# One indirect DMA for u and v of a retrieval slot, and v summed by token through 64x64 blocks of TensorE

## The reference, cut to what matters

```python
e_flat = experts.reshape(PEER_BLOCK, -1)          # 128 expert numbers a token (8 heads x 16)
u = jnp.take(expert_u, e_flat, axis=0)            # rows of 1024 floats
vv = jnp.take(expert_v, e_flat, axis=0)
act = jax.nn.gelu(jnp.einsum('td,tkd->tk', xb, u), approximate=False)
coef = (gate * act).astype(vv.dtype)
return jnp.einsum('tk,tkd->td', coef, vv)         # sum over the 128 experts of a token
# y = LayerNorm(ALPHA * x1 + PEER(x1))
```

## Time and profile before

| | us |
|---|---|
| median of 3 executions | 3767.22 |
| span of the profiled execution | 3749.1 |
| outside its span, against the median | 18.1 |

### The profile page before, as it was taken

The page is one execution under the profiler, slowest core; times in us unless marked ns, Lnnn a source line. Parts: engine busy times, 40 slices in busy tenths (PEclk is TensorE's granted clock), DMA queues, the critical chain, the costliest instruction groups (busy, mean ns, idle before and its releaser), DMA issues.

```text
span 3749.1 us, 32963 instructions
## 1 busy us (share of the span) xinstructions
PE 2448.0 (65%) x10668; PEld 1113.4 (30%) x10668; DVE 2504.2 (67%) x6614; ACT 412.7 (11%) x824; POOL 2132.7 (57%) x2180
## 2 busy tenths in 40 slices
PE   7893894656566656665566676667665555765558
PEld 5462472233123312331233232323222222431112
DVE  5188689679856886688658865887587434683331
ACT  1211211100110011001100121002100111000000
POOL 0043225666666666666566656666666556747665
PEclk8896896778668777886777778777777777768889
DMA  9998999999999999999899989999999999989998
GB/s 337 347 340 301 365 397 331 379 368 400 372 369 391 405 361 344 391 410 358 314 389 402 371 335 368 408 370 361 367 410 395 413 414 403 364 294 377 368 370 324
DMA packets 374156, 1385.50 MB, mean 370 GB/s; under 512 B 44697, under 2 KB 55577, under 8 KB 362585
## 3 DMA queue, kind: packets, MB, share of 16 engines
q0 software_dynamic: 313344, 1140.99, 79.2%
q1 hardware_dynamic: 40384, 143.04, 10.3%
q10 hardware_dynamic: 20256, 99.35, 6.9%
HBM read 1369.97 MB, written 80.18 MB: 387 GB/s over the span
## 4 chain that ended last, share of the span: by engine, by line
DVE 26%; issue 14%; PE 12%; another core or an unknown queue 11%; POOL 11%; DMA 10%; ACT 2%; ACTq 0%; POOLq 0%; DVEq 0%
DVE t L1057 11%; PE psum L1409 6%; POOL t L597 6%; DMA t<-in_expert_v,t 6%; POOL t L582 5%; DMA t<-in_expert_u,t 4%; DVE t L1003 2%; DVE t L1001 2%; DVE t L1004 2%; DVE t L1002 1%; PE psum L1271 1%; PE psum L1295 1%; DVE t L1000 1%; DVE t L1030 1%
## 5 line engine op out<-in xcount | busy, mean ns | idle before, releaser
L1409 PE MATMUL psum<-t,t 128*32 128x512 f32 x4352 | 1238.8, 786 | 729.1 <-DMA t<-in_expert_v,t 526.5
L582 POOL DMA_INDIRECT t<-in_expert_u,t x1088 | 1060.5, 975 | 923.2 <-DVE t L1057 456.8
L597 POOL DMA_INDIRECT t<-in_expert_v,t x1088 | 1072.0, 985 | 675.2 <-issue 296.7
L1057 DVE CUSTOM_DVE_ANT_0 t<-psum,t 128x1024 f32<-128x1024 f32 x928 | 1116.4, 1220 | 338.6 <-DMA t<-in_expert_u,t 260.8
L1409 PEld LDWEIGHTS psum<-t,t 128*32 128x32 f32 x4352 | 257.0, 130 | 1522.2 <-issue 1472.2
L1363 PE MATMUL psum<-t,t 128*128 128x128 f32 (+1 forms) x2304 | 314.8, 302 | 31.1 <-ACT t L736 23.6
L1363 PEld LDWEIGHTS psum<-t,t 128*128 128x128 f32 x2304 | 306.5, 217 | 80.0 <-issue 52.0
L1057 DVE CUSTOM_DVE_ANT_0 t<-t,t 128x1024 f32<-128x1024 f32 x160 | 194.5, 1222 | 168.4 <-DMA t<-in_expert_u,t 151.4
L1251 PE MATMUL psum<-t,t 128*128 128x128 f32 (+2 forms) x768 | 262.1, 501 | 7.5 <-DMA t<-in_xT 6.5
L921 DVE SCALAR_TENSOR_TENSOR t<-t,t,t 128x128 f32<-128x128 f32 x840 | 237.9, 345 | 0.2
L1271 PE MATMUL psum<-t,t 64*128 64x512 f32 (+3 forms) x192 | 118.9, 744 | 110.7 <-issue 60.6
(11 more groups left out here) (141 smaller groups left out, 1865.7 us busy)
## 6 DMA issues: line engine op xcount, KB each, us to landing
t<-in_wq_t ACTq DMA_DIRECT2D x63, 1024.0 KB
out<-in_cache_k_win SPq DMA_DIRECT2D x8, 4080.0 KB
out<-in_cache_v_win SPq DMA_DIRECT2D x8, 4080.0 KB
t<-in_w_in_t ACTq DMA_DIRECT2D x44, 512.0 KB, 7.9
t<-in_kc_t SPq DMA_DIRECT2D x8, 2560.0 KB
t<-in_vc_t SPq DMA_DIRECT2D x8, 2560.0 KB
t<-in_expert_u,t POOLq DMA_INDIRECT x1088
t<-in_expert_v,t POOLq DMA_INDIRECT x1088
```

The costliest lines, as they stand in the source:

```text
L582: pool.indirect_dma_start(u_buf[:, k % U_RING, :], None, I["expert_u"][0], bass.IndirectOffsetOnAxis(ap=idn[t % 2][:, s:s + 1], axis=0)).t ...
L597: pool.indirect_dma_start(v_buf[:, k % V_RING, :], None, I["expert_v"][0], bass.IndirectOffsetOnAxis(ap=idT[t % 3][:, tau:tau + 1], axis=0 ...
L1057: dve.tensor_tensor_reduce(out=u_buf[:, k % U_RING, :], in0=x1P if banked else x1[t % 3][:, :], in1=u_buf[:, k % U_RING, :], scale=1.0, sc ...
L1409: last = pe.matmul(bank[half][32 * j:32 * j + 32, :], zt[:, (GROUPS * t + g) % Z_RING, j, :], v_buf[:, k % V_RING, half * 512:(half + 1) * ...
```

## The change

`arrays["expert_uv"]` holds u and v of an expert side by side in HBM, rows of 8 KB. One indirect DMA a slot brings both for 128 tokens (1 MB), one token a partition. There is one ring for both, of 9 buffers of 8 KB a partition; during tile 0 only 4 of them, since the space of the others still holds the operands of the projection. A buffer comes free when TensorE has summed v of its pair of slots.

As token t's v row now lies on partition t, the sum over slots needs no reduction over partitions: the weights are diagonal. `weigh` (VectorE) writes for each slot of a pair a 128x64 tile, two stacked 64x64 identities scaled per partition by the gelu of the dot and by the gate. `values_pair` (TensorE) adds v times these weights: the blocks are 64x64, rows 0 to 63 to output partitions 0 to 63 and rows 64 to 127 to 64 to 127. In tiles 1 to 6, pairs 8 to 59, the odd slot's two blocks are crossed (rows 0 to 63 to outputs 64 to 127 and the reverse), into the two banks that are free there, and one matmul with a swap matrix puts them back at the tile's end. Gelu is taken pair by pair on ScalarE, two steps before `weigh` at the latest; `weigh` stands 2 steps, `values_pair` 3 steps behind the pair's odd slot. v of a tile is finished at the start of the next stage, the residual follows at step 6, and the stages end with a short one, n = 9. x1 has two buffers instead of three and no copy in PSUM; all dots read it from SBUF. Tile 0 has 49 dots in stage -1. The v coefficients of the first gates are taken head by head. `idT`, `coef`, the transposes for them and a round trip of the sample convolution through HBM go away. The space set aside for descriptors shrinks to 4096 bytes a partition.

```diff
+RING, FIRST_RING = 9, 4
+Z_RING = 3
...
+def slots_at(n, q):
+    early = EARLY * (PH - 1)
+    if n < 0:
+        lo, hi = (min(max(q + j - ROUTE_AT - ROUTE_STEP, 0), early) for j in range(2))
+    elif n == 0:
         lo, hi = (early + (q + j) * (SLOTS - early) // SLOTS for j in range(2))
     elif n < PT:
         lo, hi = q, q + 1
...
+        def spot(t, s):
+            if t == 0:
+                return s % FIRST_RING, s // FIRST_RING
+            k = (t - 1) * SLOTS + s
+            before = SLOTS // FIRST_RING if k % RING < FIRST_RING else 0
+            return k % RING, before + k // RING
...
+            def gather(t, s):
                 if s % TOP == 0 and t < PT:
                     pool.wait_ge(a_route, PH * t + s // TOP + 1)
                 elif s == 0:
                     pool.wait_ge(id_up, 16)
...
+                r, use = spot(t, s)
+                if t == 0:
+                    if s >= FIRST_RING:
+                        pool.wait_ge(pv, pair(0, s - FIRST_RING) + 1)
+                else:
+                    k = (t - 1) * SLOTS + s
+                    if k >= RING:
+                        pool.wait_ge(pv, pair(1, k - RING) + 1)
...
+                pool.indirect_dma_start(ring[:, r, :], None, I["expert_uv"],
+                                        bass.IndirectOffsetOnAxis(ap=idn[t % 2][:, s:s + 1], axis=0)).then_inc(landed[r], 16)
...
+            def gelu(t, p):
+                act.wait_ge(a_dot, SLOTS * t + 2 * p + 2)
+                d_ = dots[t % 2][:, 2 * p:2 * p + 2]
                 act.activation(d_, d_, ACT.Gelu).then_inc(a_gelu, 1)
...
             def dot(t, s):
-                k = ku(t, s)
-                dve.wait_ge(gu[k % U_RING], 16 * (k // U_RING + 1))
-                banked = t in P_TILES and s >= P_FROM
+                r, use = spot(t, s)
+                dve.wait_ge(landed[r], 16 * (use + 1))
                 if s == 0:
                     dve.wait_ge(x1_done, 2 * (t + 1))
...
+                dve.tensor_tensor_reduce(out=ring[:, r, 0:D], in0=x1[t % 2][:, :], in1=ring[:, r, 0:D], scale=1.0,
                                          scalar=0.0, op0=ALU.mult, op1=ALU.add, accum_out=dots[t % 2][:, s:s + 1]).then_inc(a_dot, 1)
...
+            def weigh(t, p):
+                k = PAIRS * t + p
+                dve.wait_ge(a_gelu, k + 1)
                 if k >= Z_RING:
                     dve.wait_ge(pv, k - Z_RING + 1)
+                for j in range(2):
+                    s = 2 * p + j
+                    dve.tensor_scalar(zt[:, k % Z_RING, j, :], ident2[:, :], dots[t % 2][:, s:s + 1], gtn[t % 2][:, s:s + 1],
+                                      ALU.mult, ALU.mult).then_inc(zt_ready, 1)
...
+                        q = 4 * g + i
+                        for t, p in pairs_at(n, q, 2):
+                            weigh(t, p)
+                        for s in slots_at(n, q):
+                            dot(max(n, 0), s)
+                        if n >= 1 and q == RESIDUAL_AT:
+                            residual(n - 1)
...
+                pe.wait_ge(zt_ready, 2 * (k + 1))
+                for half in range(2):
+                    for j in range(2):
+                        r, _ = spot(t, 2 * p + j)
+                        vv = ring[:, r, D + half * 512:D + (half + 1) * 512]
+                        if t == PT:
+                            last = pe.matmul(MAIN[t][half][0:NS, :], zt[:, k % Z_RING, j, :], vv, start=(p == 0 and j == 0), stop=(p == w - 1 and j == 1))
+                        elif aux and j:
+                            for a in range(2):
+                                last = pe.matmul(AUX[t][half][NS - NS * a:P - NS * a, :], zt[NS * a:NS * a + NS, k % Z_RING, j, :], vv[NS * a:NS * a + NS, :],
+                                                 start=(p == AUX_PAIRS.start), stop=(p == AUX_PAIRS.stop - 1))
+                        else:
+                            for a in range(2):
+                                last = pe.matmul(MAIN[t][half][NS * a:NS * a + NS, :], zt[NS * a:NS * a + NS, k % Z_RING, j, :], vv[NS * a:NS * a + NS, :],
+                                                 start=(p == 0 and j == 0), stop=(p == w - 1 and j == 1 and t not in AUX_TILES))
+                last.then_inc(pv, 1)
```

More of the change, by code:

```diff
@@ L140, in u_slots_at, with place, pairs_at @@
         lo, hi = q, q + 1
+    elif n == PT:
+        lo, hi = (max(0, q + j - SAMPLE_LAG) * (SLOTS // 2) // (SLOTS - SAMPLE_LAG) for j in range(2))
     else:
-        lo, hi = (max(0, q + j - 4 * LAG) * (SLOTS // 2) // (SLOTS - 4 * LAG) for j in range(2))
+        lo, hi = 0, 0
     return range(lo, hi)
+def place(n, q):
+    return SLOTS * (n + 1) + q
+PAIR_PLACE = {}
+for _n in range(-1, TILES):
+    for _q in range(SLOTS):
+        for _s in slots_at(_n, _q):
+            if _s % 2:
+                PAIR_PLACE.setdefault(place(_n, _q), []).append((max(_n, 0), _s // 2))
+def pairs_at(n, q, lag):
+    return PAIR_PLACE.get(place(n, q) - lag, [])
 def rows(n):
@@ L533, in store_y @@
                 sp.wait_ge(y_done, t + 1)
[L534 removed]
+                sp.dma_start(y_o[t * P:t * P + rows(t), :], x1[t % 2][0:rows(t), :]).then_inc(y_out, 16)
             projected_loads()
[L537 removed]
+            for n in range(TILES + 1):
                 m = n + 1
@@ new lines, in gather @@
+                if t == 0:
[5 more added lines that the diff above has]
+                        pool.wait_ge(pv, pair(1, k - RING) + 1)
+                    elif k < FIRST_RING:
+                        pool.wait_ge(pv, pair(0, SLOTS - FIRST_RING + k) + 1)
+                    elif k == FIRST_RING:
+                        pool.wait_ge(proj_done, len(UNITS))
+                        pool.wait_ge(glu_done, 3 * CT)
+                        for i in range(2):
+                            pool.wait_ge(q_out[i], 64)
@@ L612, in _ @@
+                pool.indirect_dma_start(ring[:, r, :], None, I["expert_uv"],
+                                        bass.IndirectOffsetOnAxis(ap=idn[t % 2][:, s:s + 1], axis=0)).then_inc(landed[r], 16)
+            for t in range(TILES):
+                for s in range(slots(t)):
+                    gather(t, s)
         @block.scalar
```

471 lines of the change are left out of this document (179 added, 292 removed).

## The result

The changed kernel takes 4054.57 us (median of 4 executions, 4042.86 to 4059.81) where the kernel before took 3772.76 beside it (3766.46 to 3785.14): ratio 1.0745, 95% interval 1.0717 to 1.0773. It is slower, as forecast, but by 282 us where 123 were predicted, and it lies above the range of 3790 to 3990 and above 4030 too. The profiled execution has a span of 4052.3 us, 303.2 over the earlier trace rows.

What follows compares the result with a forecast made beforehand. Steady tiles were taken as bound by transfers, VectorE close behind. 329 + 8 - 36 - 5 - 169 = +127 gave a span of 3876 us, median 3894, said as 3890; likeliest case 3790 to 3990, 8 in 10 3705 to 4030.

Steps and rivals of the forecast that it cites:

- Direction and place: Whole kernel: slower, chance 0.72, because tile 0's loop through four buffers loses 329 us.
- The sum: Tile 0's chain: a pair's v sum on TensorE takes 2.2 us at the granted clock.
- the landing: Tile 0's chain, gather to landed data: 7.0 us in stage -1, 8.5 us in stage 0.
- Clock: TensorE in tile 0: the granted 0.87 of the kernel before was used to price the v sum.
- Stage 0: Tile 0's second stretch: one-pair chain 13.2 us, two-pair 15.2; 415 us in place of 274, +141.
- Tiles 1 to 6: Steady tiles: 8 KB rows save 7.7 us a tile, 1.7 us is lost, together -36 us.
- The ring is no loss: Tiles 1 to 6: nine buffers suffice, as the loop takes about 14 us where four pairs last 21.
- Tile 7: Tile 7: -7.7 us for 8 KB rows, about +3 where routing fills VectorE, together -5 of 495.
- The end: From tile 8's first dot to the end of the span: 204 us in place of 373, -169.
- Rival 1: Whole kernel not slower: tile 0 loses under 200 us and the DMA gains more; 3635 or 3700 us, chance 0.20.
- Rival 3: v sums: straight blocks do not run side by side, +1.9 us in tile 0's chain; 4010 us, chance 0.12.
- the tenth of a microsecond: Tile 0's chain: dots reading x1 from SBUF slow a GpSimd gather by 0.1 us.

Runs made afterwards that it cites:

- experiment 2: Changed kernel, but in tile 0 the v sum leaves out the odd slot of each pair, 8 records instead of 16: 3964.53 us.
- experiment 6: Changed kernel plus six zero-weight TensorE matmuls ahead of each wait for the weights of pairs 1 to 24 of tile 0, in stage -1: 4040.71 us.
- experiment 12: Changed kernel with the last pass of the projection summing only one of eight k steps: 4046.06 us.
- experiment 5: Changed kernel with tile 0 slot by slot: each slot weighed, summed and its buffer freed by itself; 3774.60 us, ratio 1.0557 to the kernel before.

## Why the prediction was wrong, step by step

- **Direction and place: right.** Tile 0's loop through four buffers is the loss, with the predicted order and releasers. The DMA share is 0.49 in stage -1 where I had said about 0.6. Tile 0 took 909.7 us, over even the 906 that all the upper bounds together gave.
- **The sum, the step that failed.** "The v sum: eight matmuls of 512 columns ... four sets of two: 1.9 us, or 3.6 at half clock." I read the x16 of the earlier trace rows as sixteen matmuls, and they are the records of eight. So each of the four sets of two takes two records one after the other, 0.86 us instead of 0.43: 3.65 us a pair at the full clock, 6.55 nearly all at half, 5.59 on the mean of stage -1. The earlier trace rows was misread too: its four records start at 1210.08, 1210.10, 1210.51 and 1210.53, two by two 0.43 us apart, which is the full clock. Against 2.2 the sum is 3.4 us longer in 24.5 pairs, +83 us; the landing, 5.85 instead of 7.0, takes 28 back. The net +55 is the stage's miss (368 against 314). In experiment 2 the sum with 8 records takes tile 0 to 817 us and the time to 3964.53, inside the range.
- **Clock.** I carried the granted 0.87 of before over to a TensorE that now idles 144 of the stage's 368 us. It was 0.78, and experiment 6 shows the idling to be the cause. Taken at 0.87 in the way of the prediction, 3.65 us would be 4.2; so of the 3.4 us about 2.0 are the records and 1.4 the clock (an estimate), 49 and 34 us of the stage.
- **Stage 0, +119** (541.7 for 415 + 8, the restart being 9.8 for 8). "Three pairs take both once: 28.4 / 3 = 9.5 us." The share was near (15 of 35 pairs behind the even dot), both chains were too short: 17.9 and 11.1 us a pair for 13.2 and 7.6. In the 15 pairs the sum takes 4.27 us for 2.2 and the landing 7.43 for 8.5, and the weights wait 3.21 us for TensorE, which works on the projection and the front, where the prediction had 0.3 for a hand-over and gave no reason to leave the queue out. Half the sum is worth 43 us in this stage (experiment 2). How the other 76 divide was not shown: experiment 12 takes 1.5 us a pair off that wait, and the stage gains only 9 us, because sum and landing become longer.
- **Tiles 1 to 6, -17 instead of -36.** "The ring is no loss" was wrong: one buffer less costs 29 us a tile, a sum one step earlier gives 8.3. What works against it is the rate where buffers are free, 412 GB/s in tile 8 and not 382. That the two errors have opposite signs and so bring the total near the forecast is luck; what each is worth in these tiles was not taken apart. The crossed sums are mostly hidden as said, though a pair takes 1.95 us at the full clock and 2.45 on the mean, not 1.0 to 1.9.
- **Tile 7, +10 instead of -5.** TensorE has 382 us of 505 instead of 294 of 495, since 64 straight pairs have 8 records more than priced. That this is what made the tile longer is argued, not shown: experiment 5 has 494.8 us with the same code for it. Sums and weights a step earlier bring it to 487 to 491.
- **The end, -201 instead of -169:** 155.8 us to the last dot instead of 188 (176 and 12 of idle DMA). The rate was higher and the DMA did not idle (share 1.00); 9 of the 64 gathers were issued before tile 8's first dot. Behind the last dot stand 16.2 us, as said.
- **Rivals.** Rival 1 needed tile 0 to lose under 200 us. It is out even with the sum as priced: experiment 2 loses 418 there. Steady tiles took 376.0 us, not the 360 of its better DMA. **Rival 3** (straight blocks one after the other) is false: the two blocks of a set start 2 to 39 ns apart, and sixteen records take 3.65 us where sixteen of the projection, one after the other, take 7.03. Its price, 96 us for a sum 1.9 us longer, was nearly what the sum's error cost in place of it. The Trainium skill (TensorEngine Tiling (Array Packing), "Gotcha 1: PSUM Pressure") says that different row tiles cannot access one bank at the same time. The trace disagrees for these blocks, which write different partitions of the bank.
- **GpSimd: no wait in tile 0, a long one elsewhere.** A gather takes 1.106 us on the mean, where the two kinds before took 0.975 and 0.985, but in tile 0 it takes 0.94 and 0.98: there only 3 of 124 gathers start inside a dot with more than 0.2 us of it left. So the tenth of a microsecond did not come in tile 0's chain. From tile 1 on many gathers start inside a dot, and then the gather waits for the dot to end. The rule of the Trainium skill (SBUF — State Buffer, "Who interferes with whom") that I set aside, that the loser is blocked for the whole instruction, shows in the single instructions:

```profile
1430.53 1.22 DVE L1036 CUSTOM_DVE_ANT_0 t<-t,t 128x1024 f32<-128x1024 f32 x1
1430.55 2.01 POOL L603 DMA_INDIRECT t<-in_expert_uv,t  x1 [0.30 <-issue]
```

```profile
1004.56 1.22 DVE L1057 CUSTOM_DVE_ANT_0 t<-psum,t 128x1024 f32<-128x1024 f32 x1
1004.80 0.94 POOL L597 DMA_INDIRECT t<-in_expert_v,t  x1 [3.90 <-remote]
```

The first two lines are the changed kernel, the other two the kernel before, with x1 in PSUM. Over the whole traces: 393 gathers of the changed kernel start inside a dot and take 1.38 us on the mean, up to 2.01, and where more than 0.2 us of the dot is left, 305 of 318 take that rest and 0.81 us more. In the kernel before, 701 start inside a dot that reads x1 from PSUM and take 0.94; 87 start inside one that reads it from SBUF (tile 7 above all) and take 1.53. The tenth of a microsecond of the prediction was a mean over gathers with and without such a dot. What these waits cost tiles 1 to 7 was not measured.

## What to carry to other kernels

Count a line's records against the matmuls of the program before a price is read from them. Here the factor of two stood in a link of a loop, and halving that link took 92 us off tile 0 (experiment 2).

When a buffer is given back only behind a second consumer, write the loop out in each engine's order and ask which instruction stands behind one that waits for the buffer. One step of position gave 182 us, smaller pieces another 104, and no arithmetic was saved. Count the queue in front of each link too: 3.4 us a pair stood there in stage 0. Then shorten the hold only where the producer is ready, since the same step in all tiles cost 10 us a tile in waits for gelu, and moving the sums alone gave 8.

A mean over instructions that meet different neighbours hides a wait. Sort them by what runs beside them before a rule is set aside.
